# Second expert layer: one gather for the token rows of two experts, and two weight slots that can be filled in the stage in front

## What is computed

```python
def ec_moe(h, w_router, w_gate, w_up, w_down):
    cap = EC_CAPACITY * n // N_EXPERTS                  # 64 tokens for each of 16 experts
    aff = jax.nn.softmax((h @ w_router).astype(F32), axis=-1)
    gate, idx = lax.top_k(jnp.swapaxes(aff, 1, 2), cap)
    xs = h[bidx, idx]
    hid = jax.nn.silu(jnp.einsum('becd,edf->becf', xs, w_gate)) * jnp.einsum('becd,edf->becf', xs, w_up)
    y = jnp.einsum('becf,efd->becd', hid, w_down) * gate.astype(h.dtype)[..., None]
    return jnp.zeros_like(h).at[bidx, idx].add(y)
```

## Time and profile before

| | us |
|---|---|
| median of three runs | 4130.43 (4124.16 to 4131.09) |
| the profiled execution, whole | 4126.45 |
| its span in the trace | 4124.7 |
| TensorE busy | 3729.0 (90%) |
| VectorE busy | 2043.9 (50%) |
| the routing stage and second expert layer, in the span | about 2274 to 2812 |

### The profile page before, as it was taken

The page is one execution under the profiler, slowest core; times in us unless marked ns, Lnnn a source line. Parts: engine busy times, 40 slices in busy tenths (PEclk is TensorE's granted clock), DMA queues, the critical chain, the costliest instruction groups (busy, mean ns, idle before and its releaser), DMA issues. The chain is left out here.

```text
span 4124.7 us, 66951 instructions
## 1 busy us (share of the span) xinstructions
PE 3729.0 (90%) x28462; PEld 2446.8 (59%) x28462; DVE 2043.9 (50%) x4045; ACT 872.6 (21%) x2050; POOL 407.6 (10%) x460
## 2 busy tenths in 40 slices
PE   6989989987999969898898698888999999999998
PEld 3477478762444435565787243344368878468877
DVE  3766765553222226575746333333464455664455
ACT  3153244320000021432631000002320002440001
POOL 0042033001111110420500000000000000000000
PEclk9999999988999989899999799998999999999999
DMA  6312401138999951312220999992112222132221
GB/s 245 137 39 88 163 18 54 67 145 326 391 393 391 405 168 41 103 42 86 79 102 32 373 405 407 409 414 103 41 67 82 81 95 85 41 107 82 72 92 56
DMA packets 166360, 673.12 MB, mean 163 GB/s; under 512 B 13416, under 2 KB 26920, under 8 KB 141488
## 3 DMA queue, kind: packets, MB, share of 16 engines
q1 hardware_dynamic: 154656, 649.84, 41.1%
q0 software_dynamic: 9984, 16.78, 1.8%
q10 hardware_dynamic: 1424, 2.23, 0.2%
HBM read 651.80 MB, written 17.02 MB: 162 GB/s over the span
## 5 line engine op out<-in xcount | busy, mean ns | idle before, releaser
L3977 PE MATMUL bank<-weight_ring_extra_b,xs_b 128*32 128x512 f32 x2544 | 281.8, 593 | 7.8 <-DMA weight_ring_extra_b<-in_moe_in 7.5
L3977 PE MATMUL bank<-weight_ring,xs_b 128*32 128x512 f32 x1936 | 220.1, 605 | 13.3 <-DMA weight_ring<-in_moe_in 6.9
L4069 ACT ACTIVATE moe_silu_b<-bank 128x256 f32<-128x256 f32 x80 | 25.5, 383 | 959.7 <-PE bank L3977 959.7
L3086 PE MATMUL bank<-heads_out_b,swiglu_sums_b 128*128 128x256 f32 x1008 | 224.4, 379 | 0.0
L4080 DVE TENSOR_SCALAR xs_b<-bank,factor_b,mod_b 128x64 f32<-128x64 f32 (+1 forms) x384 | 95.4, 324 | 230.2 <-PE bank L3961 230.2
L3086 PEld LDWEIGHTS bank<-heads_out_b,swiglu_sums_b 128*128 128x128 f32 x1008 | 191.5, 190 | 26.0
L3977 PEld LDWEIGHTS bank<-weight_ring_extra_b,xs_b 128*32 128x32 f32 x2544 | 79.6, 110 | 183.7 <-issue 175.7
L4121 DVE TENSOR_TENSOR heads_out_b<-heads_out_b,bank 128x256 f32<-128x256 f32 x256 | 90.1, 414 | 159.1 <-PE bank L4014 159.1
L4034 PE MATMUL bank<-weight_ring_extra_b,moe_hidT_b 128*32 128x256 f32 x2784 | 155.6, 381 | 8.3 <-DMA weight_ring_extra_b<-in_moe_down 6.7
L2470 PE MATMUL bank<-hT_b,token_block_sums_b 128*128 128x256 f32 x608 | 143.1, 389 | 15.7 <-DVE hT_b L2604 15.7
L3086 PE MATMUL bank<-hT_b,weight_ring 128*128 128x256 f32 x672 | 151.9, 379 | 0.0
(11 more groups left out here) (615 smaller groups left out, 7577.7 us busy)
## 6 DMA issues: line engine op xcount, KB each, us to landing
weight_ring_extra_b<-in_moe_in SPq DMA_DIRECT2D x60, 2048.0 KB, 24.6
weight_ring<-in_moe_in SPq DMA_DIRECT2D x48, 2048.0 KB, 24.7
weight_ring_extra_b<-in_moe_down SPq DMA_DIRECT2D x33, 2048.0 KB, 25.8
weight_ring<-in_ada_w SPq DMA_DIRECT2D x24, 2048.0 KB, 8.0
weight_ring<-in_moe_down SPq DMA_DIRECT2D x21, 2048.0 KB, 26.1
weight_ring<-in_ssd_w_in SPq DMA_DIRECT2D x12, 2048.0 KB, 8.1
hT_b<-in_moe_in SPq DMA_DIRECT2D x10, 2048.0 KB, 41.9
weight_ring<-in_ffn_w_gate SPq DMA_DIRECT2D x10, 2048.0 KB, 7.7
```

The source lines that it names most:

```text
L3086: last = pe.matmul(out, lhs[:, k, :], rhs[:, k, :], start=(k == 0), stop=(k == HK - 1))
L3977: last = pe.matmul(in_bank(g)[lanes[c], :], xs[:, e % 2, kt, g * GROUP:(g + 1) * GROUP], w[:, k, :, c * COLS:(c + 1) * COLS], start=(kt == 0),
L4069: last = act.activation(sl[:, g, :], in_bank(g)[:, 0:COLS], ACT.Silu)
```

## The change

- `Ring.feed` no longer stops at an entry without a transfer for want of its slot.
- The list gives expert load 0 to slot 6 and load 1 to slot 7, then the ring's own three slots, then 3, 4, 5 and 8 (`AHEAD`). The round is still nine slots.
- Slots 6 and 7 are now the two halves of one buffer, `room`, which lives through the whole second layer: the SSD scan keeps its inputs there, the gate projection its block sums, and after the gate projection the ring is told that they are free, so that loads to them can start in the output projection.
- To make room for that, other buffers of the output projection move: the normed rows `xn` and block sums into the old `hT` and `heads_out`, the squares into a buffer of their own. Later layers take their block sums from a half of `room`.
- In the second expert layer the index of expert 2j + i stands in column j of `slot_rows`, at partitions 64 i to 64 i + 63. `fetch_two(j)` gathers the 128 rows of the experts 2j and 2j + 1 by one transfer, into one of two halves that now use all 128 partitions: eight gathers instead of sixteen. The pair j is issued when expert 2j - 3 has been turned.

```diff
@@ Ring.feed
-            if (before is not None and before > end) or slot - self.slots >= len(self.extra):
+            if (before is not None and before > end) or (self.loads[n] and slot - self.slots >= len(self.extra)):
                 break
@@ route
-            pe.transpose(core.bank[3][0:used, 0:NE], place[0:NE, :], core.ident[0:NE, 0:NE])
+            pe.transpose(core.bank[3][0:copies * used, 0:NE], place[0:NE, :], core.ident[0:NE, 0:NE])
...
+            if copies == 2:
+                dve.tensor_copy(place[0:NE, used:], place[0:NE, 0:used])
...
-            dve.tensor_copy(rows[0:used, :], core.bank[3][0:used, 0:NE])
             if slot_tokens is None:
+                dve.tensor_copy(rows[0:used, :], core.bank[3][0:used, 0:NE])
                 dve.tensor_copy(row_parts[:], turned_rows)
             else:
+                for i in range(2):
+                    here = slice(i * used, (i + 1) * used)
+                    dve.tensor_copy(rows[here, 0:NE // 2], core.bank[3][here, i:NE:2])
                 dve.tensor_copy(slot_tokens[:], turned_rows)
@@ moe
+AHEAD = ((), (3, 4))
...
+            def fetch_two(j):
+                if j >= 2:
+                    pool.wait_ge(tokens_turned, 2 * j - 2)
+                pool.indirect_dma_start(got[:, j % 2, :], None, core.h_dram,
+                                        bass.IndirectOffsetOnAxis(rows[:, j:j + 1], 0)).then_inc(fetched[j % 2], 16)
...
+                if X is None:
+                    mine, side = slice(0, slots), e % 2
+                    pe.wait_ge(fetched[side], 16 * (e // 2 + 1))
+                else:
+                    mine, side = slice(e % 2 * slots, (e % 2 + 1) * slots), e // 2 % 2
+                    pe.wait_ge(fetched[side], 16 * (e // 4 + 1))
...
-                    last = pe.transpose(bank[:, at:at + slots], got[0:slots, e % 2, k * P:(k + 1) * P], core.ident[0:slots, 0:slots])
+                    last = pe.transpose(bank[:, at:at + slots], got[mine, side, k * P:(k + 1) * P], core.ident[mine, mine])
@@ plan
-        slots += [ring.slots + n for n in range(EXPERT_SLOTS[layer])]
+        extra = [ring.slots + n for n in range(EXPERT_SLOTS[layer])]
+        slots = [extra[n] for n in AHEAD[layer]] + slots + [x for n, x in enumerate(extra) if n not in AHEAD[layer]]
@@ ssd_layer, after the gate projection
+        core.ring.extra = [None] * AHEAD[1][0] + [room[:, 1], room[:, 0]]
...
-        xn = core.sb(own, "xn", TX, D)
-        squares = hT[:].rearrange("p k n -> p (k n)")[:, 4 * HALF_K * 256:4 * HALF_K * 256 + D]
+        free = hT[:].rearrange("p k n -> p (k n)")
+        later = kept[:, TX * D:]
+        xn = free[:, 0:TX * D].rearrange("p (t n) -> p t n", t=TX)
+        S = parts_of(later, KT, 2) + parts_of(free[:, TX * D:], KT, 1)
+        squares = core.sb(own, "squares", D)[:]
```

More of the change, by code:

```diff
@@ L2329, in as_block_sums, with parts_of @@
     return x.rearrange("p a b -> p (a b)")[:, 0:4 * HALF_K * 256].rearrange("p (i k n) -> p i k n", i=4, n=256)
+def parts_of(x, k, count):
+    n = NX // 2
+    return [x[:, i * k * n:(i + 1) * k * n].rearrange("p (k n) -> p k n", k=k) for i in range(count)]
 def begin_plain(core, pe, src, name, tile, side, count):
@@ L2363, in gemm_seven @@
             block, token_sums, weight_sums, plain, product, combined, first_copied, moved, link, *tail_sems):
-        S = core.sb(own, "token_block_sums", 3, src.shape[1] // 2, half)
+        S = [core.sb(own, f"token_block_sums{n}", src.shape[1] // 2, half)[:] if x is None else x for n, x in enumerate(S)]
         C = core.sb(own, "product_parts", 2 if on_scalar else 1, 7, HN)
@@ L2935, with __init__ @@
 class BlockHeads(Heads):
-    def __init__(self, core, own, kept, y, yT, gate):
+    def __init__(self, core, own, kept, y, yT, gate, junk):
         super().__init__(core, own, y, yT, gate, 1, TC)
@@ L2943, in __init__ @@
         self.inv = kept
-        self.junk = core.sb(own, "row_junk", 512)
+        self.junk = junk
     def start_scalar(self, act, part):
@@ L3726, in route @@
         found = own.enter_context(core.nc.sbuf_tensor(f"found_{layer}", [P, used], U32))
-        place = core.sb(own, "place", used)
+        copies = 1 if slot_tokens is None else 2
+        place = core.sb(own, "place", copies * used)
         place_parts = core.sb(own, "place_parts", groups, TILES, GROUP)
@@ L3813, in _ @@
                                              float(row), None, ALU.add))
-            slots_of = (x[0:NE].rearrange("p (g i) -> p g i", i=GROUP) for x in (place, best))
+            if copies == 2:
+                dve.tensor_copy(place[0:NE, used:], place[0:NE, 0:used])
+            slots_of = (x[0:NE, 0:used].rearrange("p (g i) -> p g i", i=GROUP) for x in (place, best))
             places, bests = slots_of
@@ L3925, in fetch @@
                                         bass.IndirectOffsetOnAxis(rows[0:slots, e:e + 1], 0)).then_inc(fetched[e % 2], 16)
-            fetch(0)
-            fetch(1)
-            if X is not None:
+            def fetch_two(j):
[4 more added lines that the diff above has]
+            if X is None:
+                fetch(0)
+                fetch(1)
+            else:
+                fetch_two(0)
+                fetch_two(1)
                 for c in range(TILES):
@@ L3932, in _ @@
                               allow_small_or_imprecise_dtypes=True).then_inc(numbered, 1)
-            for n in range(NE + 2):
+                for j in range(2, NE // 2):
+                    fetch_two(j)
+            for n in range(NE + 2 if X is None else 0):
                 if n + 2 < NE:
@@ L3936, in _ @@
                     fetch(n + 2)
-                if n >= 2 and X is None:
+                if n >= 2:
                     e = n - 2
@@ L4812, in program @@
             kept = core.sb(second_layer, "heads_out", TX * SI)
-            ssd_layer(core, kept[:])
+            room = core.sb(second_layer, "normed_and_mixed", 2, SLOT)
+            hT, catT = (room[:, n].rearrange("p (k n) -> p k n", k=KT) for n in range(2))
+            ssd_layer(core, kept[:], room[:])
             X, M = (kept[:, n * TX * D:(n + 1) * TX * D].rearrange("p (t n) -> p t n", t=TX) for n in range(2))
[L4815 to L4821, removed]
+            moe_layer(core, 1, list(range(TC, TT)), kept[:, TX * D:].rearrange("p (k n) -> p k n", k=KT),
+                      [room[:, 1], room[:, 0], kept[:, TX * D:TX * D + SLOT]], X)
+            normed_by = second_start(core, X, M, hT, catT)
+            second_rest(core, X, M, hT, normed_by, out, room[:, 1])
         core.clear_ended()
```

41 lines of the change are left out of this document (23 added, 18 removed).

## The result

| | before | after |
|---|---|---|
| median of five runs | 4125.62 (4123.12 to 4131.09) | 4098.36 (4091.82 to 4106.98) |
| the profiled execution | 4126.45, span 4124.7 | 4098.36, span 4096.6 |

The ratio of the times is 0.9932 (95% interval 0.9917 to 0.9946): 27 us faster (22 to 34). The forecast was 4112 with a range from 4102 to 4124. The direction was right, the gain was larger than the range allowed.

The account below looks back on a forecast made before the run. The prediction took the second expert layer to be bound by its stream of weights. Loads ahead (5.3 us) and fewer gathers (10.6) summed to 15.9; 4128 - 16 gave 4112, range 4102 to 4124.

Parts of the forecast that it names:

- What bounds the layer: Second expert layer: bound by the stream of weights, DMA share 0.99 to 1.02, last load landing at 2788.1.
- rival 3: Nothing moves: last expert's spread and joins set the layer's end, or another part gives back the gain; 4128, chance 0.08.
- Two slots filled ahead, 5.3 us: Start of second expert layer: four loads go early, first gather meets a near-empty queue, load 9 lands 5.3 us earlier (0 to 6.5).
- rival 2: The preload counts in full, without a standstill: 19.8 + 10.6 = 30.4 us, 4098; chance 0.04.
- Eight gathers instead of sixteen, 10.6 us: Behind load 9, six gathers of 128 rows at 3.0 replace 13 of 64 at 2.2: 10.6 us (2.2 to 15.4).
- cost by the gather alone: Low end for a 128-row gather's price in the second expert layer: 2.2 us, the same as for 64 rows.
- the best ends: Largest gains of the two terms, 6.5 + 15.4 = 21.9 us, giving 4106 before the runs' spread.
- Rivals 1 and 4: Second expert layer's gathers: (1) cost by rows, 4.4 each, 4120.5, chance 0.14; (4) wide gather holds stream whole flight, 4154, 0.08.
- rival 1: Second expert layer: a gather costs by its rows, so six cost 4.4 us each; 4120.5, chance 0.14.
- Edits with no price: Later slots for `ev_v`, `ev_k`, `final_gain`, moved buffers and odd experts' transposes cost nothing; an uncovered `ev_k` would cost 8.4 us.
- The pace: Second expert layer: experts under gathers 31.3 us apart instead of 32.0, in pairs 62.5.
- the second term: The gain from fewer, wider gathers behind load 9 in the second expert layer: 10.6 us (2.2 to 15.4).

Follow-up runs that it names:

- ahead_only: Changed kernel with the loads ahead kept, but back to one gather of 64 rows for each expert; median 4124.95, ratio to before 0.9986.
- rows96: Changed kernel with one gather per expert, from expert 2 on of 96 rows on partitions 0 to 95; weight stream 451.1 us, 2.39 a gather.

## Why the prediction was right or wrong

**What bounds the layer: right.** Both kernels' whole layer is the stream; the halves of the change nearly add up in it (16.7 + 6.6 = 23.3 of 24.5) without anything else taking over. TensorE didn't become the bound behind load 9; rival 3 is out. From 2400 to 2500 of the kernel after TensorE is busy all the time, since it still has full slots in front of it; the transfers run at 426 GB/s meanwhile, so the stream loses nothing there.

**Two slots filled ahead, 5.3 us: right in its mechanism and near in size.** The loads went out as drawn, four ahead of the layer, five together, then a standstill. The gather landed after 4.5 us (5.0 taken, between 4.2 and 10.0). Load 9 was issued 112.58 and 110.95 us behind the router's weights in the two runs, before 116.97 and 118.46: 6.0 us earlier on average, against 4.7 forecast. Its landing took 8.7, not the 8.0 to 8.4 of the forecast, so the 0.6 us that the empty queue was to give load 9 itself didn't come. ahead_only puts the whole term at 6.6 from the layer's lengths. The preload counting in full (rival 2) didn't come; that its 4098 is the measured time is chance.

**Eight gathers instead of sixteen, 10.6 us: the step that failed.** From the landing of load 9 to that of the last load, before took 2788.1 - 2333.7 = 454.4 us; after, 2314.25 + 8.7 = 2322.95 and 2717.62 + 40.2 = 2757.8 make 434.9: 19.5 us less instead of 10.6. By prices, 13 x 2.05 - 6 x 1.29 = 18.9. The 2.2 of 64 rows was close to the 2.00 to 2.08 found here. What failed was the value for 128 rows: 3.0, with ends 2.2 and 4.4, where 1.29 was measured. The prediction read the rows for 64 and 96 as a fixed part plus bytes and went on along this line to 128. The price of 96 rows that it drew from the landings' drift, 2.8, was of the right order (2.39 in rows96). But 32 rows cost half of 64, so there is no fixed part, and 128 rows aren't on the line at all: merging paid because a transfer over all partitions costs hardly more than its bytes (1.29 against 1.23), not because a fixed part fell due less often. Its lower end, "cost by the gather alone", let nothing be cheaper than a narrow gather, and no row excluded that; a bound at the bytes alone, 1.2 us, would have put the best ends at 6.5 + 28.6 - 7.2 = 27.9 and the range's low end, by the same steps, at about 4096.

The estimate from the Trainium skill ("DMA: Bandwidth & Descriptors", section "Anatomy of one DMA — SWDGE (gpsimd) path"), 3.2 us for 128 rows, missed in the same way. The other reading that the prediction drew from that section of the Trainium skill, that the fixed part of 2.0 us is a latency and a full queue loses only the bytes, agrees with the 1.29 of 128 rows, and disagrees with the 1.95 to 2.08 of 64.

**Rivals 1 and 4** both went by a wide gather that costs more than a narrow one: 4.4 us or a whole flight. With 1.29 both are out. Between 32 and 64 rows the price does go by the rows (1.05 and 2.05), as rival 1 had it for all sizes; 128 break the rule.

**Edits with no price: right** as far as the layer's length tells, since it is near the sum of the two halves. Behind the layer 1313.6 stands in three of the four runs of the two kernels (1312 to 1317 in all thirteen), so `ev_k` and `final_gain` cost nothing that can be seen.

**The pace.** Experts were to be 31.3 us apart. With the measured price it is 6 x 4.96 + 1.29 / 2 = 30.4, and ScalarE's four experts from 2530.8 to 2652.4 after, in which two gathers lie, are 30.4 apart. Ahead of them the full slots let TensorE run at its own 27.0.

**From 4112 to 4098.** Of the 13.6 us of the miss, 8.9 are the second term (19.5 against 10.6) and 1.3 the first (6.6 against 5.3). Another 2.4 are the base: the forecast subtracted from 4128.0, while the five runs of the kernel before beside the result have their median at 4125.62. An execution's part ahead of the layer moves by more than what is left. The miss isn't that part's doing: the layer alone, 23.3 and 25.6 us shorter, already gains more than the 15.9 of the forecast.

## What to carry to other kernels

Where a stream of weights bounds a stage, judge small transfers beside it by what they take from the stream, not by their bytes or their landing: give them all 128 partitions in one transfer, by merging two requests or by cutting rows into halves. A DMA share of 1.0 isn't a stream at its best; compare GB/s with a stretch that has no other transfer. And don't bound an unseen size by a line through two sizes that share a property (both left partitions empty) which the new one lacks.

## What was not expected of the hardware

A transfer of 112 rows of 4 KB cost the stream beside it 2.75 us, one of 128 rows 1.29, and the same 262 KB cost 0.70 us on 128 partitions and about 2 on 64, there with indices (2.00 to 2.08) and without (1.95). During the gathers of 64 and 112 rows the packets of the weights' queue took 679 to 693 ns on average instead of 544 to 557. The price of narrow transfers rises with their rows, 1.05, 2.05, 2.39, 2.75 for 32, 64, 96 and 112, not in proportion at the end. Counts between 112 and 128, rows spread otherwise over the partitions, and what makes the weight packets slower, stay open.
